# Attention of a decoder step: compressed sample keys scored as raw key pages, key pages loaded in eight joint groups between the projection tiles, no GpSimd multiplies

## What is computed

```
past_cmp = kv_pool[page_table, :, 0:2]              # 8 pages of 128 rows per sample: k_cmp, v_cmp
w = softmax(pos_w, axis=1)                          # one weight per position in a block of 64
kvc = einsum('bnlckd,clk->bnckd', blocks, w)        # compressed keys kc, values vc: one per block
s_c = einsum('btkrd,bnkd->btkrn', q, kc) - slope * dist_c
p_c = masked_softmax(s_c, ...);  o_c = p_c @ vc
idx = top_k(p_c summed over the group)              # which blocks of k_sel, v_sel are attended
o = gate0 * o_c + gate1 * o_selected + gate2 * o_window
```

## Time and profile before

| | us |
|---|---|
| three timed runs: median (lowest, highest) | 1052.1 (1051.12, 1054.39) |
| the profiled execution | 1056.31 |
| its span from first to last instruction | 1054.2 |
| TensorE busy in the span | 999.7 (95%) |
| VectorE busy | 491.0 (47%) |
| GpSimd busy | 187.8 (18%) |

### The profile page before, as it was taken

One profiled execution on the slowest core, in us unless ns is written; L12 is line 12 of the kernel. 1 busy time (PEld: TensorE's weight loads), 2 busy tenths in 40 slices (PEclk: granted clock), 3 DMA queues, 4 the chain that ended last, 5 costly groups with the idle time before them and its releaser, 6 DMA issues. The chain is left out here.

```text
span 1054.2 us, 14961 instructions
## 1 busy us (share of the span) xinstructions
PE 999.7 (95%) x5177; PEld 624.7 (59%) x5177; DVE 491.0 (47%) x1422; ACT 334.2 (32%) x875; POOL 187.8 (18%) x201
## 2 busy tenths in 40 slices
PE   8999999899999999998899977979999999999897
PEld 6888776788744444443678854544875444444366
DVE  2889797871611111111379986671153111112046
ACT  3212888710451111110340013572044211112134
POOL 0000016311120000000345542441103000000033
PEclk9999999999899999999999986998998999999999
DMA  9963787779669999999727995959985999999974
GB/s 324 315 214 130 225 271 248 250 240 404 272 273 427 427 427 426 426 426 428 302 93 271 377 352 168 305 169 368 427 335 214 426 427 426 425 427 426 426 301 205
DMA packets 90144, 343.20 MB, mean 326 GB/s; under 512 B 15890, under 2 KB 53906, under 8 KB 73170
## 3 DMA queue, kind: packets, MB, share of 16 engines
q1 hardware_dynamic: 80074, 319.48, 78.2%
q10 hardware_dynamic: 7688, 18.39, 4.9%
q0 software_dynamic: 2304, 4.33, 1.2%
HBM read 331.56 MB, written 23.04 MB: 336 GB/s over the span
## 5 line engine op out<-in xcount | busy, mean ns | idle before, releaser
L1522 DVE TENSOR_TENSOR gates_and_hidden<-bank,gates_and_hidden 128x512 f32<-128x512 f32 x16 | 11.1, 692 | 311.4 <-PE bank L1173 311.4
L1173 PE MATMUL bank<-expert_ring,x_packed 128*64 128x512 f32 x320 | 118.6, 607 | 0.0
L1154 PE MATMUL bank<-expert_ring,x_packed 128*64 128x512 f32 x416 | 112.7, 593 | 0.9 <-DMA expert_ring<-in_moe_w_gate 0.9
L559 PE MATMUL ss<-xT,expert_ring 128*128 128x264 f32 x384 | 89.5, 393 | 4.4 <-DMA expert_ring<-in_ssd_w_in 4.4
L559 PEld LDWEIGHTS ss<-xT,expert_ring 128*128 128x128 f32 x384 | 73.1, 193 | 18.3 <-DMA xT<-in_xT 4.4
L1154 PEld LDWEIGHTS bank<-expert_ring,x_packed 128*64 128x64 f32 x416 | 36.6, 137 | 73.3 <-issue 73.3
L1383 POOL DMA_INDIRECT x_rows_packed<-x_rows,slot_token_int x16 | 16.4, 1023 | 339.3 <-DVE gates_and_hidden L1487 293.4
L1517 DVE TENSOR_TENSOR acc<-acc,bank 128x264 f32<-128x264 f32 x128 | 55.0, 429 | 39.1 <-PE bank L1210 37.5
L1765 PE MATMUL bank<-xT,expert_ring 128*128 128x264 f32 (+1 forms) x324 | 72.5, 386 | 0.3 <-PEq L1006 0.3
L1195 PE MATMUL bank<-expert_ring,gates_and_hidden 128*64 128x512 f32 x256 | 70.8, 595 | 1.4 <-ACT gates_and_hidden L1344 1.4
L1765 PEld LDWEIGHTS bank<-xT,expert_ring 128*128 128x128 f32 (+1 forms) x324 | 60.2, 187 | 12.5 <-issue 1.0
(11 more groups left out here) (417 smaller groups left out, 1840.3 us busy)
## 6 DMA issues: line engine op xcount, KB each, us to landing
expert_ring<-in_moe_w_gate SPq DMA_DIRECT2D x26, 2048.0 KB, 19.8
expert_ring<-in_moe_w_up SPq DMA_DIRECT2D x18, 2048.0 KB, 20.0
expert_ring<-in_moe_w_down SPq DMA_DIRECT2D x16, 2048.0 KB, 20.0
expert_ring<-in_ssd_w_in SPq DMA_DIRECT2D x9, 2048.0 KB, 8.7
expert_ring_b<-in_moe_w_gate SPq DMA_DIRECT2D x6, 2048.0 KB, 17.8
expert_ring_c<-in_moe_w_up SPq DMA_DIRECT2D x6, 2048.0 KB, 22.5
expert_ring_d<-in_moe_w_up SPq DMA_DIRECT2D x6, 2048.0 KB, 21.0
expert_ring_c<-in_moe_w_down SPq DMA_DIRECT2D x6, 2048.0 KB, 22.5
```

The costliest lines, as they stand in the source:

```text
L559: last = mm(pt[m % 4][:, 0:T], wc[:, k, ((m - 1) % 4) * P:((m - 1) % 4 + 1) * P], xT[:, k, :], start=k == 0, stop=k == KD - 1)
L1154: last = mm(hb[0][s * CAP:(s + 1) * CAP, :], xg[:, k, s * CAP:(s + 1) * CAP], unit(6 * i + s)[:, k * FF:(k + 1) * FF], start=k == 0, stop= ...
L1173: last = mm(hb[1][s * CAP:(s + 1) * CAP, :], xg[:, k, s * CAP:(s + 1) * CAP], unit(6 * i + 2 + s)[:, k * FF:(k + 1) * FF], start=k == 0, s ...
```

## The change

- The cache is laid out anew: `vcmp_pages` holds the values to be compressed alone (a page is now 128 KB), `k_pages` holds compressed-branch keys and selected keys of a page side by side (256 KB).
- Samples' compression is for values only: two multiplies and two sums a sample, all on VectorE. GpSimd multiplies nothing of it.
- Keys come in eight groups of eight pages, 2 MB each. `dec_keys(j)` scores both kinds: 16 matmuls of 32x256. It runs between the projection tiles: after tile 8 groups 0 and 1, then one after tiles 9, 10, 12, 13, 14 and 15. The compressed scores are then multiplied by the position weights and summed over 64 positions (`key_half`).
- The position weights come by a new constant, `pos_rows`, whose Exp stands on ScalarE ahead of its copy of tile 4; its maximum, on VectorE, waits for all twelve constants. `bias_win` goes.
- The gates become tile 16 of 21; the prompt's compressed scores go up behind tile 18. From tile 8 on the tiles use two PSUM banks in turn.
- All page loads of the block are SyncE's. Each group's page numbers are read anew just ahead of it (`read_pages`); before, the numbers for values of even samples were kept from the earlier reads.
- A sixth 2 MB buffer, `ring_e`, is added for attention, and the order of the first expert weights of layer 1 is another.

```diff
@@ load_cmp
-                sp.dma_start(cmp_buffer(b)[:, n], I["cmp_pages"][bass.ds(page[b * NPG + n], 1)]...).then_inc(ld_cmp[cmp_slot(b)], 16)
+                sp.dma_start(cmp_buffer(b)[:, n], I["vcmp_pages"][bass.ds(page[b * NPG + n], 1)]...).then_inc(ld_cmp[b % 6 // 2], 16)
@@ attention
-            KV_SLOT = (1, 2, 0, 3, 4, 1, 2, 0, 3, 4, 1, 2)
+            KV_SLOT = (5, 0, 1, 2, 5, 0, 1, 2, 5, 0, 1, 2, 4, 3, 5, 0)
+            NKEY, KWIN, VAL = 8, 8, 10
+            KEYS_AT = {8: (0, 1), 9: (2,), 10: (3,), 12: (4,), 13: (5,), 14: (6,), 15: (7,)}
+            def read_pages(sp, j):
+                if j < NKEY:
+                    t, first, n = j % 2, 2 * (j // 2), 2
+                else:
+                    t, first, n = (j - VAL) // 3, 4 * ((j - VAL) % 3), 4
+                pages[j] = [page_number(sp, (2 * g + t) * NPG + first + q) for g in range(4) for q in range(n)]
@@ SyncE
+                    page = {n: page_number(sp, n) for n in range(4 * NPG, 6 * NPG)}
+                    load_cmp(sp, 4, page)
+                    load_cmp(sp, 5, page)
+                    for dst, n in (... twelve constants, the last "nsa_w_gates"):
+                        sp.dma_start(dst[:], I[n]).then_inc(ld_nc, 16)
+                    page = {n: page_number(sp, n) for n in range(6 * NPG, 8 * NPG)}
+                    sp.wait_ge(c_used, 2)
+                    load_cmp(sp, 6, page)
+                    load_cmp(sp, 7, page)
+                    read_pages(sp, 0)
+                    load_kv(sp, 0)
+                    for j in range(1, 4):
+                        read_pages(sp, j)
+                        sp.wait_ge(c_used, 2 * j + 2)
+                        load_kv(sp, j)
+                    for j in range(4, VAL + 2):
+                        if j < NKEY or j >= VAL:
+                            read_pages(sp, j)
+                        sp.wait_ge(kv_used, j - 3)
+                        load_kv(sp, j)
@@ GpSimd
-                    for b in range(1, DB):
-                        pool.wait_ge(ld_cmp[cmp_slot(b)], 16 * NPG * (b // 3 + 1))
-                        for a in range(2, 4):
-                            cmp_multiply(nc.gpsimd, b, a).then_inc(c_mult, 1)
@@ TensorE
-                        k5 = kv_buf[s].rearrange("p (g q c t) -> p g q c t", g=4, q=4, c=2)
+                        k5 = kv_buf[s].rearrange("p (g q c t) -> p g q c t", g=4, q=2, c=4)
+                        for kind, bk in enumerate((pt[4 + a], dp[a])):
...
+                    for m in range(NT):
+                        tile(m)
+                        for j in KEYS_AT.get(m, ()):
+                            dec_keys(j)
+                        if m == GATES:
+                            score(0)
+                        elif m == GATES + 2:
+                            cmp_scores()
+                            turn_gates()
+                    score(1)
+                    turn_new_values()
+                    turn_cmp_prompt()
@@ ScalarE
-                        if m in (4, 8, 12):
-                            load_batch({4: 3, 8: 5, 12: 7}[m])
+                        if m == 4:
+                            act.wait_ge(row_max, 1)
+                            A_(pos_row[:], pos_row[:], ACT.Exp, bias=pos_stat[:, 0:1], accum_out=pos_stat[:, 1:2]).then_inc(row_exp, 1)
@@ VectorE
+                    compress(0)
+                    compress(1)
+                    dve.wait_ge(ld_nc, 16 * 12)
+                    V.tensor_reduce(pos_stat[:, 0:1], pos_row[:], AX.X, ALU.max, negate=True).then_inc(row_max, 1)
+                    for b in range(2, DB):
+                        compress(b)
+                    spread_queries()
```

More of the change, by code:

```diff
@@ L1024, in _ @@
                         if L == 0:
-                            page = [page_number(sp, n) for n in range(2 * NPG)]
+                            page = {n: page_number(sp, n) for n in range(2 * NPG)}
                         if L == 1:
@@ L1042, in _ @@
                                 load_chunk(sp, c, I["nsa_w_in"][c])
+                            page = {n: page_number(sp, n) for n in range(2 * NPG, 4 * NPG)}
                             sp.wait_ge(e_done, 4)
-                            load_cmp(sp, 1, page)
+                            load_cmp(sp, 2, page)
+                            load_cmp(sp, 3, page)
                         if out is not None:
@@ L1673, in load_kv @@
-            def load_kv(eng, j, page):
-                for g in range(4):
-                    load_kv_group(eng, j, g, page)
+                if KWIN <= j < VAL:
+                    for g in range(4):
+                        sp.dma_start(kv_buf[s][:, g * 1024:(g + 1) * 1024].rearrange("p (c t) -> p c t", c=2), I["kwin"][2 * g + j - KWIN]).then_inc(ld_kv[s], 16)
+                elif j >= VAL and (j - VAL) % 3 == 2:
+                    for g in range(4):
+                        sp.dma_start(kv_buf[s][:, g * 1024:(g + 1) * 1024].rearrange("p (a c) -> p a c", a=4), I["vwin"][2 * g + (j - VAL) // 3]).then_inc(ld_kv[s], 16)
+                else:
+                    table, n = ("k_pages", 2) if j < NKEY else ("vsel_pages", 4)
+                    for i, page in enumerate(pages[j]):
+                        src = I[table][bass.ds(page, 1)].rearrange("a p c -> (a p) c")
+                        sp.dma_start(kv_buf[s][:, i * CH // (4 * n):(i + 1) * CH // (4 * n)], src).then_inc(ld_kv[s], 16)
@@ L1693, in _ @@
-                    read_pages(6)
-                    sp.wait_ge(c_used, 4)
-                    load_cmp(sp, 6, page)
-                    read_pages(0)
-                    def read_odd(half):
-                        for b in range(1, DB, 2):
-                            for n in range(4):
-                                page[b * NPG + 4 * half + n] = page_number(sp, b * NPG + 4 * half + n)
-                    sp.wait_ge(c_used, 6)
-                    load_kv(sp, 0, page)
-                    sp.wait_ge(tile_done, d0 + 16)
@@ L1898, in turn_dec_out, with cmp_scores @@
                         last.then_inc(o_turned, 1)
-                    pe.wait_ge(tile_taken, t0 + NT - 3)
-                    score(0)
-                    vt = (V_SEL, V_SEL + 1, V_WIN, V_WIN + 1)
-                    pe.wait_ge(tile_taken, t0 + NT - 1)
-                    for q in range(QT):
+                    def cmp_scores():
+                        pe.wait_ge(kc_ok, 2)
+                        pe.wait_ge(kc_read, 2)
+                        csv = pt[4][:, 0:QT * AH * 4].rearrange("p (x f r n) -> p x f r n", x=4, f=2, r=4)
+                        for i in range(KD):
+                            for q in range(QT):
+                                last = mm(csv[:, 2 * q + i // 4, :, i % 4, :], qT[:, i, q * P:(q + 1) * P], kcx[:, i // 4].rearrange("p f n -> p (f n)"), start=True, stop=True)
+                        last.then_inc(csc, 1)
@@ L2020, in exps @@
+                        c = (n + 1) // 4 + 1
+                        if m != GATES and (n + 1) % 4 == 0 and 2 <= c < nchunk:
+                            load_chunk(act, c % 2, I["nsa_w_in"][c])
                     def exps(u):
@@ L2090, in _, with spread_queries @@
-                    i1.then_inc(c_used, 1)
+                        cmp_sum(V, kcd, b, 1).then_inc(c_used, 1)
+                    def spread_queries():
+                        dve.wait_ge(q_zero, 1)
+                        dve.wait_ge(tile_taken, t0 + KD)
+                        for p in range(2):
+                            for half in range(2):
+                                r = slice(64 * half, 64 * half + 64)
+                                i1 = V.tensor_copy(qbd[r, p, :].rearrange("q (b c) -> q b c", c=144)[:, :, 8 * p + 4 * half:8 * p + 4 * half + 4],
+                                                   qT[r, 4 * p:4 * p + 4, SEQ:T].rearrange("q r b -> q b r"))
+                        i1.then_inc(q_ok, 1)
@@ L2121, in soft @@
+                    key_half(0)
+                    prompt_blocks()
+                    take_half(0)
+                    key_half(1)
+                    take_half(1)
                     def soft(u):
```

347 lines of the change are left out of this document (153 added, 194 removed).

## The result

The changed kernel takes 1104.7 us (median of 4 runs, 1103.1 to 1106.4), the kernel before, measured beside it, 1051.6 us. The ratio is 1.053, with a 95% interval from 1.049 to 1.057. The profiled executions have spans of 1103.4 and 1054.2 us. The forecast was 1092 us (1071 to 1112), so the direction and the kind are right and the time is 12.7 us above its middle.

What follows compares the result with a forecast made beforehand. VectorE's compressions held the loop's start before; SyncE's page reads and issues would after. +44.2 us to the loop, -6.5 in it and +2.9 for the clock gave 1052.1 + 40.6 = 1092.7, said as 1092 us (1071 to 1112).

Steps and rivals of the forecast that it cites:

- Constants 8.4: SyncE's list before the key groups: issuing twelve constants takes 8.4 us, between bounds of 5.2 and 12.5.
- A key group 8.5: SyncE during the projection: eight reads and eight loads per key group, 4.57 + 3.94 = 8.5 us; eight groups 68.1.
- Landing 3.1: After SyncE's last key issue at 660.9: the pages land 3.1 us later (median, to 13.5), at 664.0.
- the third rival: SyncE's page issues: full DMA engines stretch eighty loads to 0.73 us instead of 0.49, +19 us, 1111 us; chance 14%.
- Behind the last keys 29.6: TensorE between key group 7's landing and the loop: last keys, five tiles, scores, gates and transposes take 29.6 us.
- 2.9 for the clock: TensorE behind key group 7: one fall to a slow clock adds 2.9 us.
- ScalarE, VectorE and the PSUM banks are beside this: Between the last keys and the loop: these add no time to TensorE's 29.6 us.
- The loop, -6.5: In the loop: four key pieces go, saving between 4.3 and 8.7 us, taken as 6.5.
- From the loop's end, 0.: Behind the loop to the kernel's end: all as before, only 38 to 41 us later, so no change.
- Keys come in time: Projection: SyncE keeps ahead, TensorE takes 97.6 us to the loop, -7.9 us in all, 1044 us; chance 6%.
- The queries are late: Before the first keys: queries, behind all eight compressions, hold TensorE instead of pages; +21.5 us, 1074 us; chance 12%.
- the prediction's sign of being wrong: Projection: TensorE's first key wait being released by VectorE would mean late queries and refute the forecast; no size given.

Runs made afterwards that it cites:

- Experiment 1: Changed kernel without reads of page numbers: page i taken for table entry i, so the page table's content is left out; 1078.4 us, ratio 1.030.
- experiment 7: Changed kernel with key groups 1, 3, 5 and 7 read and issued by ScalarE between its tile copies; 1090.6 us, ratio 1.039.
- experiment 8: Changed kernel with one unchecked load per set of page numbers, odd key groups on ScalarE, queries spread and ScalarE's first exponentials done earlier; 1079.6 us, ratio 1.029.
- experiment 9: Changed kernel with one unchecked load per set of page numbers, early queries, early exponentials, and SyncE as the only issuer; 1072.4 us, ratio 1.022.
- experiment 3: Changed kernel with ScalarE's first exponentials moved ahead of its last two tile copies; 1100.6 us, ratio 1.047.
- Experiment 12: Kernel before with only 5 of every 16 matmuls of the samples' selected keys, the rest of that product left out; 1055.1 us, ratio 1.005.
- experiment 4: Changed kernel with one load for a whole set of page numbers, each number's range check kept; 1091.8 us, ratio 1.042.
- experiment 5: Changed kernel with single reads of page numbers but no range checks; 1089.1 us, ratio 1.037.
- experiment 10: Kernel before with all samples' multiplies on VectorE and one unchecked load per set of page numbers on both issuing engines; 1045.2 us, ratio 0.9964.
- experiment 2: Kernel before with every multiply of the samples' compression on VectorE, none on GpSimd; ratio 1.001.

## Why the prediction was right, and where its sizes were off

*SyncE's list is the path: shown.* The first keys were released by the transfer of `k_pages`, 56.4 us into the projection, and so were all later ones that TensorE waited for. The start of the loop came 27.7 us earlier without reads, 21.6 with reads of 0.30 us instead of 0.56, and 16.5 with a second reader and issuer. Experiment 1 also moves other pages than the table names; the other two move the right ones and point the same way. The Trainium skill (DMA: Bandwidth & Descriptors, section Issuing engines are not separate DMA queues) says that several issuers save only sequencer time, usually small beside the DMA. That it is sequencer time agrees with experiment 7; that it is small does not, with 16.5 us. In experiments 8 and 9, where the reads were gone, a second issuer saves nothing at all.

*The terms of that list.* Sixteen reads 9.1: measured 8.9 and 9.0. Sixteen loads 7.9: 8.5 and 8.8. Constants 8.4: 7.0. A key group 8.5: 8.8. Landing 3.1: 4.65 for the last group. Together keys 7 start at 117.6 us where the sum had 113.6, **+4.0**. The sum counts its loads rightly (16 + 16 + 64), but the upper end of the range and the third rival take eighty for these 96: at their prices the range would be 2 us wider upwards, and the rival 1116 us instead of 1111.

*Behind the last keys 29.6, and 2.9 for the clock.* Measured 36.7, **+4.2** over both. The clock term was near: two tiles and the prompt's scores lost 3.5 us (9.87 and 4.27 instead of 7.2 and 3.5). The step that failed within the right mechanism is "ScalarE, VectorE and the PSUM banks are beside this": the 4.84 us wait for `v_new` is theirs (it has no term in the sum), and experiment 3 took 3.8 us of it away by moving ScalarE's exponentials. ScalarE's and VectorE's timelines of the changed kernel show the chain:

```profile
690.20 0.39 ACT L2031 ACTIVATE expert_ring_c<-bank 128x264 f32<-128x264 f32 x1 [3.17 <-PE bank L1781]
690.61 1.28 ACT L2041 ACT_TABLE_LOAD   x1
...
692.99 0.17 DVE L2165 RECIPROCAL row_scale<-row_sum 128x2 f32<-128x2 f32 x1 [12.33 <-ACT gates_and_hidden L2042]
...
697.04 0.67 DVE L2235 COPY v_new<-bank 8x512 f32<-8x512 f32 x1
```

The last tile's copy comes first, a table load behind it, then the exponentials, for which VectorE waits 12.33 us, and its copy of `v_new` comes 4 us later still.

*The loop, -6.5.* Measured -3.0, **+3.5**; seven of the nine traces of the changed kernel's family have 86.2 to 87.3 us there, two 89.8 and 90.6. The term was mis-sized, and the rows that I had gave its lower bound, 4.2, too high: the first pairs without keys took 5.8, 4.8 and 4.1 us (14.7 together), not three times 3.84, as they run at a low clock (granted 0.68, 0.64 and 0.60) and wait for VectorE (1.57 and 0.70 us in the first). TensorE's timeline of the changed kernel, first matmuls of these pairs:

```profile
704.56 0.49 PE L1790 MATMUL bank<-expert_ring_c,expert_ring_b 64*128 64x128 f32 x4 [0.70 <-DVE neg_max L2159]
...
709.36 0.80 PE L1790 MATMUL bank<-expert_ring_c,expert_ring_b 64*128 64x128 f32 x4
```

The fourth pair starts at 713.48. Experiment 12 gives 3.3 us in the kernel before's loop for two thirds of the keys' work.

*From the loop's end, 0.* +2.8 in this pair of traces, inside the scatter of that stretch over all kernels. With -5.9 ahead of the projection the spans differ by 49.2 us, 8.6 more than the sum's 40.6. The medians differ by 53.1: the profiled execution of the kernel before was 4.7 us above its median, that of the changed kernel 0.5. From the projection on every stretch missed upwards. What was luck is inside SyncE's list, where the constants were 1.4 us cheaper than the sum had them and hid part of the dearer loads, and the -5.9, which no term had and which brings the spans nearer together than the stretches behind it do.

*The rivals.* "Keys come in time" failed at the reads. "The queries are late" is true as the next bound: it took over in experiments 1, 4, 5 and 7, and in experiment 3 too, whose list up to the first keys is that of the changed kernel. In the changed kernel it stayed hidden by 0.2 us. So the prediction's sign of being wrong, a first wait that VectorE releases, does not tell the two apart: both chains come out of SyncE's list, and what tells them apart are the later groups, for which TensorE waits by DMA. In experiment 3 too TensorE waits for transfers behind it (4.48 us before the next keys), so the queries are caught up there, as the prediction says. Its time of 1074 was 4 below experiment 1: the constants landed sooner than it assumed (there VectorE's wait for them ends 7.2 us after the last of them was issued, not 13.8), and the last stretch and the loop were longer. "Issues are stretched" happened on a small scale: 0.53 to 0.55 us a sample page load instead of 0.49.

*What stays open:* why experiment 12 is slower as a whole; what the scatter of about 5 us to either side behind the output projection is; how much faster experiment 10 really is; and what fewer or smaller page transfers would be worth where the DMA engines are full, which no run tried.

## What to carry to other kernels

Add up the list of the engine that issues transfers as you would a compute engine's: each page number that it reads and each load that it issues took 0.56 and 0.5 us here. Neither counts as busy time, and the timeline lists only the loads; the reads show as gaps, or when one asks for their line. When data is to be used earlier, count what its issuer must have done by then, not how busy the DMA engines are. And once that list is short, look for the next holder before adding an issuer: here these were the queries, the buffers and the full DMA engines.

## What the runs showed of the hardware

- A read of one number into a register of SyncE, one of sixteen in a row, took 0.56 us with its range check and 0.30 us without (experiment 5). The load itself is 0.27 us (median). The Trainium skill (DMA: Bandwidth & Descriptors, section Latency and other measured facts) gives a floor of about 600 ns for a tensor load; the loads here, from a table in SBUF, are below it.
- One load of sixteen neighbouring numbers took 1.1 to 1.2 us (experiment 8), one load of eight numbers that lie apart 1.95 us (experiment 9, 572.28 to 574.23). The load instruction itself is 0.97 us of the one and 1.71 us of the other.
- The issue of a page load took 0.49 us for 128 KB (7.82 us for sixteen in experiment 1, from 546.26) and for 256 KB (3.94 us for eight) alike; while the DMA engines were full it took up to 0.91 us (7.28 us for eight in experiment 2, from 587.31).
- Four VectorE multiplies of 128x1024 took 4.62 us alone (experiment 2), two beside GpSimd's multiply 4.50 us.
- While the DMA engines were full (share 1.03 to 1.08) they moved 365 to 432 GB/s in experiment 10 between 583.5 and 606.3 us, and a 256 KB page issued then landed 7.5 to 18.4 us after its issue.
